# A five-layer network on one core: state-space read-out by 128-row products, and three feed-forward layers that norm behind their first product

## What is computed

```python
def rmsnorm(x, g):
    y = xf * rsqrt(mean(xf * xf, axis=-1) + EPS) * g

def conv_gated_ffn(xn, w_up, conv_w, conv_b, w_down):      # layers 0 to 3; xn = rmsnorm(x, g)
    h = causal_depthwise_conv(xn @ w_up, conv_w, conv_b)   # 3 taps over the tokens
    a, g = split(h, 2)
    return (silu(g) * a) @ w_down                          # ffn4 is the same without the convolution

# s5_layer: the scan gives the states xr, xi of 64 groups; then
y  = einsum('ghp,blgp->blgh', c_re, xr) - einsum('ghp,blgp->blgh', c_im, xi) + d_skip * u
hg = gelu(y) @ w_glu
```

## Time and profile before

| | |
|---|---|
| median of 3 runs | 1708.34 us (1707.26 to 1709.61) |
| the profiled execution's own time | 1710.79 us |
| its span in the profile | 1709.0 us |
| instructions | 29919 |
| mean granted clock of PE | 0.996 of full speed |
| PE, DVE, ACT, POOL busy | 97%, 66%, 53%, 18% |

### The profile page before, as it was taken

One profiled execution on the slowest core, in us unless ns is written; L12 is line 12 of the kernel. 1 busy time (PEld: TensorE's weight loads), 2 busy tenths in 40 slices (PEclk: granted clock), 3 DMA queues, 4 the chain that ended last, 5 costly groups with the idle time before them and its releaser, 6 DMA issues.

```text
span 1709.0 us, 29919 instructions
## 1 busy us (share of the span) xinstructions
PE 1661.0 (97%) x12900; PEld 1529.0 (89%) x12900; DVE 1130.8 (66%) x1578; ACT 904.7 (53%) x1212; POOL 312.7 (18%) x377
## 2 busy tenths in 40 slices
PE   8999999999999998999999999999999999999998
PEld 7989999898999987789998897999988898899998
DVE  5657689856775678567666665766676776645455
ACT  6555554544556657465545555645553755443434
POOL 1212799501370001000000011101006200000000
PEclk9999999999999999999999999999999999999999
DMA  7445547464554554345555433755555632555551
GB/s 253 140 138 171 183 162 247 160 219 148 175 174 158 168 197 140 132 158 188 196 177 170 150 133 112 208 189 181 191 171 153 194 113 90 167 191 182 191 179 49
DMA packets 203395, 286.20 MB, mean 167 GB/s; under 512 B 6432, under 2 KB 162272, under 8 KB 203264
## 3 DMA queue, kind: packets, MB, share of 16 engines
q1 hardware_dynamic: 197584, 272.25, 48.6%
q0 software_dynamic: 2224, 5.75, 1.4%
q10 hardware_dynamic: 3456, 6.29, 1.1%
HBM read 279.03 MB, written 5.24 MB: 166 GB/s over the span
## 4 chain that ended last, share of the span: by engine, by line
PE 89%; DVE 6%; ACT 2%; issue 2%; POOL 1%; DMA 0%; ACTq 0%; SPq 0%; POOLq 0%; DVEq 0%
PE ps L107 88%; DVE wlo L119 2%; ACT arena L113 1%; PE ps L110 1%; ACT whi L113 1%; DVE xres L119 1%; POOL sm L119 1%; DVE arena L119 1%; DVE arena L125 1%; DVE arena L122 0%; DVE sm L122 0%; DVE arena L128 0%; DVE ol L119 0%; DVE arena L137 0%; DMA xres<-in_x 0%
## 5 line engine op out<-in xcount | busy, mean ns | idle before, releaser
L119 DVE TENSOR_TENSOR wlo<-raw,whi 128x2048 fp32r<-128x2048 f32 (+2 forms) x259 | 602.1, 2330 | 259.0 <-ACT whi L113 258.9
L107 PE MATMUL ps<-xh,whi 128*128 128x256 f32 x2296 | 654.7, 285 | 3.8 <-DVE wlo L119 2.4
L107 PE MATMUL ps<-xh,wlo 128*128 128x256 f32 x2296 | 650.5, 283 | 0.0
L107 PE MATMUL ps<-xl,whi 128*128 128x256 f32 x2296 | 650.4, 283 | 0.0
L113 ACT ACTIVATE whi<-raw 128x2048 fp32r<-128x2048 f32 (+2 forms) x259 | 491.9, 1901 | 245.8 <-PE ps L107 242.9
L107 PEld LDWEIGHTS ps<-xh,whi 128*128 128x128 f32 x2296 | 440.3, 192 | 11.0 <-issue 5.0
L107 PEld LDWEIGHTS ps<-xl,whi 128*128 128x128 f32 x2296 | 440.5, 192 | 2.0 <-issue 0.2
L107 PEld LDWEIGHTS ps<-xh,wlo 128*128 128x128 f32 x2296 | 440.3, 192 | 0.1
L107 PE MATMUL ps<-whi,oh 128*128 128x512 f32 (+1 forms) x640 | 249.4, 390 | 0.7 <-ACT arena L113 0.7
L107 PE MATMUL ps<-wlo,oh 128*128 128x512 f32 (+1 forms) x640 | 247.4, 387 | 0.0
L107 PE MATMUL ps<-whi,ol 128*128 128x512 f32 (+1 forms) x640 | 246.8, 386 | 0.0
(11 more groups left out here) (152 smaller groups left out, 1668.6 us busy)
## 6 DMA issues: line engine op xcount, KB each, us to landing
raw<-in_ffn_w_up SPq DMA_DIRECT2D x88, 1024.0 KB, 5.1
raw<-in_ffn_w_down SPq DMA_DIRECT2D x44, 1024.0 KB, 4.9
raw<-in_sb_w_qkv SPq DMA_DIRECT2D x23, 1024.0 KB, 5.5
raw<-in_w_ffn_in SPq DMA_DIRECT2D x22, 1024.0 KB, 5.1
raw<-in_w_in SPq DMA_DIRECT2D x19, 1024.0 KB, 5.1
raw<-in_w_ffn_out SPq DMA_DIRECT2D x11, 1024.0 KB, 5.0
raw<-in_sb_w_o SPq DMA_DIRECT2D x8, 1024.0 KB, 4.9
raw<-in_sg_w_in SPq DMA_DIRECT2D x8, 1024.0 KB, 5.3
```

The costliest lines, as they stand in the source:

```text
L107: return NOP if self.e is None else self.e.matmul(*a, **k)
L119: return NOP if self.e is None else self.e.tensor_tensor(*a, **k)
```

## The change

**Read-out.** y is kept in another order: rows are the four time steps i times 32 features, and the four groups of channels qq stand along the columns. So one product with 128 columns of weights takes the place of four with 32: `read_out` has 4 products with `toep` and 16 with the states. The gelu puts the order right: `gelu(n)` is 16 instructions on 32 rows and 2x64 elements. `gelu(1)` moves from ahead of group 3's work on ACT to behind it, and the load of table `toep` 2 moves up.

**Feed-forwards 2, 3 and 4.** The raw residual is turned (`raw_turn_pe`, 16 transpositions), eight of them ahead of the last bank's sums, four ahead of the first tile and four within it. ACT makes the high parts (`raw_high_act`), DVE the low parts (`raw_low_dve`), the first four ahead of its last addition. The banks are now finished in the order (0,0), (1,0), (0,1), (1,1). The norm's factors are made beside the first tiles; two products turn them into a row (`raw_scale_pe`), ACT copies it, and DVE multiplies each bank of each block by it (`up_scaled`, two instructions of 128x512 a block). The taps read that product and not PSUM, and ACT's first tap waits for it; PE takes a bank again as soon as it is scaled.

The diff, cut to its core:

```diff
@@ feat_major_pair
         for k in range(KT):
+            if st in self.RAW and k == 2:
+                self.raw_turn_pe(pe, st, 1, 1)
             pe.wait_ge(*self.on("xl", st, k))
@@ into_residual
+        if final and st in self.RAW_AFTER:
+            nxt = self.RAW_AFTER[st]
+            for t, j in ((0, 0), (1, 0), (0, 1), (1, 1)):
+                if t == j == 1:
+                    pe.wait_ge(*self.on("x_new", nxt, 1, 0))
+                    for tt in range(2):
+                        self.raw_turn_pe(pe, nxt, tt, 0)
+                part(0, t, j)
+                ins = part(1, t, j)
...
@@ add_residual
+        if nxt in self.RAW:
+            for t, j in ((0, 0), (1, 0), (0, 1), (1, 1)):
+                xs, b = self.x[:, t, j * 512:(j + 1) * 512], self.B[4 + 2 * t + j]
+                if t == j == 1:
+                    self.raw_low_dve(dv, nxt, 0)
+                dv.wait_ge(*(self.on("tile", *key) if t == j == 1 else self.on("sum", st, t, j)))
+                dv.tensor_tensor(xs, b[:, :], xs, ALU.add).then_inc(*self.up("x_new", nxt, t, j))
+            self.raw_low_dve(dv, nxt, 1)
+            return
@@ new
+    RAW = {"ffn2": 40, "ffn3": 56, "ffn4": 72}
+    RAW_AFTER = {"stick1": "ffn3", "second": "ffn4"}
+    def raw_turn_pe(self, pe, st, t, j):
+        pe.wait_ge(*self.on("x_new", st, t, j))
+        for kt in range(4 * j, 4 * j + 4):
+            b, c = self.raw_at(st, kt)
+            ins = pe.transpose(b[:, c + t * P:c + (t + 1) * P], self.x[:, t, kt * P:(kt + 1) * P], self.ident[:, :])
+            if t:
+                ins.then_inc(*self.up("x_turned", st, kt))
+    def raw_high_act(self, ac, st, j):
+        for kt in range(4 * j, 4 * j + 4):
+            b, c = self.raw_at(st, kt)
+            ac.wait_ge(*self.on("x_turned", st, kt | 1))
+            ac.activation(self.xh[:, kt, :], b[:, c:c + 256], ACT_F.Copy, scale=self.gcol(self.RAW[st] + kt)).then_inc(*self.up("xh", st, kt))
+    def raw_low_dve(self, dv, st, j):
+        for kt in range(4 * j, 4 * j + 4):
+            b, c = self.raw_at(st, kt)
+            dv.wait_ge(*self.on("xh", st, kt | 1))
+            dv.scalar_tensor_tensor(self.xl[:, kt, :], b[:, c:c + 256], self.gcol(self.RAW[st] + kt), self.xh[:, kt, :].bitcast(F32),
...
@@ raw_act
+        self.raw_high_act(ac, st, 0)
+        squares(0, 0)
+        squares(1, 0)
+        squares(0, 1)
+        self.raw_high_act(ac, st, 1)
+        squares(1, 1)
@@ raw_scale_pe
+        for t in range(2):
+            pe.wait_ge(*self.on("scaled", st, t))
+            ins = pe.matmul(self.B[3][:, t * P:(t + 1) * P], self.nones[:, :], self.diag(st)[:, t, :], start=True, stop=True)
@@ ffn_pe
+                    if raw and blk == s == 1:
+                        pe.wait_ge(*self.on("r_out", st))
+                    if raw and blk >= 2:
+                        pe.wait_ge(*self.on("up_scaled", l, blk - 2, s))
...
+                    if raw and blk == s == 0:
+                        self.raw_turn_pe(pe, st, 0, 1)
...
+            if raw and blk == 0:
+                self.raw_scale_pe(pe, st)
@@ ffn_act
-                    ac.wait_ge(*self.on("tile", "up", l, s, blk))
+                    ac.wait_ge(*(self.on("up_scaled", l, blk, s) if raw else self.on("tile", "up", l, s, blk)))
@@ ffn_dve
+            if raw and blk == 0:
+                self.cut_lo(dv, ("up", l, 1, 0), 0)
+                self.raw_sums_dve(dv, st)
+                self.cut_lo(dv, ("up", l, 0, 0))
+                self.raw_diag_dve(dv, st)
...
+            if raw and blk < NB:
+                for s in range(2):
+                    dv.wait_ge(*self.on("tile", "up", l, s, blk))
+                    dv.wait_ge(*self.on("r_out", st))
...
+                    dv.tensor_tensor(self.up_scaled()[:, 2 * s:2 * s + 2, :], self.up_bank(blk, s),
+                                     self.raw_scale().unsqueeze(1).to_broadcast([P, 2, 256]), ALU.mult).then_inc(*self.up("up_scaled", l, blk, s))
@@ read_out
-            for i in range(4):
-                for qq in range(4):
-                    pe.matmul(y(qq, i), toep[:, qq, i, :], U4[:, j, qq, :], start=i == 0, stop=False, skip_group_check=True)
+            for qq in range(4):
+                pe.matmul(y(qq), toep[:, qq, :, :].rearrange("p i n -> p (i n)"), U4[:, j, qq, :], start=qq == 0, stop=False, skip_group_check=True)
...
-                    for i in range(4):
-                        for qq in range(4):
-                            ins = pe.matmul(y(qq, i)[:, 1:64], xc[c].rearrange("p a g h -> p a (g h)")[:, 4 * qq + i, :], src[:, qq, c, 0:63],
+                    for qq in range(4):
+                        ins = pe.matmul(y(qq)[:, 1:64], xc[c][:, 4 * qq:4 * qq + 4, :, :].rearrange("p a g h -> p (a g h)"), src[:, qq, c, 0:63],
@@ s5_pe, last tiles
+            if hf:
+                pe.wait_ge(*self.on("x_new", "ffn2", 1, 0))
+                for t in range(2):
+                    self.raw_turn_pe(pe, "ffn2", t, 0)
             glu(hf, 0, 1)
@@ s5_act
-            ac.activation(yT, B[2 + n % 2][:, :].rearrange("p (a b) -> p a b", b=256), ACT_F.Gelu_apprx_tanh).then_inc(*self.up("y_gelu", n))
+            out = yT.rearrange("p a (c i) -> p a c i", i=4)
+            for i in range(4):
+                for qq in range(4):
+                    ins = ac.activation(out[32 * qq:32 * qq + 32, :, :, i], self.s5_y2(n)[32 * i:32 * i + 32, :, qq, :], ACT_F.Gelu_apprx_tanh)
+            ins.then_inc(*self.up("y_gelu", n))
...
-            if j == 3:
-                gelu(1)
...
-            if j % 2 and j != 3:
+            if j % 2:
                 gelu(j // 2)
```

More of the change, by code:

```diff
@@ L401, in part @@
                             w[0][:, k, j * 512:(j + 1) * 512], w[1][:, k, j * 512:(j + 1) * 512], first and k == 0, final and k == 1)
+        if final and st in self.RAW_AFTER:
[7 more added lines that the diff above has]
+                ins = part(1, t, j)
+                if (t, j) != (1, 1):
+                    ins.then_inc(*self.up("sum", st, t, j))
+            ins.then_inc(*self.up("tile", *key))
+            return
         if final:
@@ L481, in gains_dve, with raw_at @@
         dv.tensor_copy(self.gt[:, 0:64], self.B[0][:, 0:64]).then_inc(*self.up("gains"))
+    RAW = {"ffn2": 40, "ffn3": 56, "ffn4": 72}
+    RAW_AFTER = {"stick1": "ffn3", "second": "ffn4"}
+    def raw_at(self, st, kt):
+        return self.B[((4, 5, 6, 7) if st == "ffn2" else (4, 6, 5, 3))[kt // 2]], kt % 2 * 256
+    def raw_turn_pe(self, pe, st, t, j):
[5 more added lines that the diff above has]
+                ins.then_inc(*self.up("x_turned", st, kt))
@@ new lines, in raw_act, with squares @@
+    def raw_act(self, ac, st):
+        ss = self.small("ss" + st, 5)
+        ac.wait_ge(*self.on("gains2" if self.RAW[st] >= 64 else "gains"))
+        def squares(t, j):
+            c = slice(j * 512, (j + 1) * 512)
+            ac.wait_ge(*self.on("x_new", st, t, j))
+            ac.activation(self.jk[:, t, c], self.x[:, t, c], ACT_F.Square, accum_out=ss[:, 2 * t + j:2 * t + j + 1]).then_inc(*self.up("squared", st, t, j))
+        self.raw_high_act(ac, st, 0)
[4 more added lines that the diff above has]
+        squares(1, 1)
@@ L486, with raw_scale_pe, raw_scale @@
+    def raw_scale_pe(self, pe, st):
+        for t in range(2):
+            pe.wait_ge(*self.on("scaled", st, t))
+            ins = pe.matmul(self.B[3][:, t * P:(t + 1) * P], self.nones[:, :], self.diag(st)[:, t, :], start=True, stop=True)
+        ins.then_inc(*self.up("r_turned", st))
+    def raw_scale(self):
+        return self.ar[:, 5120:5376]
     NORM_BANKS = {"stick0": (4, 5, 0, 1, 2, 3, 6, 7), "stick1": (4, 5, 0, 1, 2, 3, 6, 7), "s5": (4, 5, 0, 1, 2, 3, 6, 7),
@@ L2834, in scalar @@
         self.s5_act(ac)
-        self.norm_act(ac, "ffn2", 40)
+        self.raw_act(ac, "ffn2")
         self.ffn_act(ac, 2)
@@ L2839, in scalar @@
         self.stick_act(ac, "stick1")
-        self.norm_act(ac, "ffn3", 56)
+        self.raw_act(ac, "ffn3")
         self.ffn_act(ac, 3, self.nsa_prep_act(ac))
@@ L2863, in vector @@
         self.s5_dve(dv, "ffn2")
-        self.turned_dve(dv, "ffn2", 40)
         self.ffn_dve(dv, 2, "stick1")
@@ L2887, in tensor @@
         self.s5_pe(pe)
-        self.norm_pe(pe, "ffn2")
         self.ffn_pe(pe, 2)
@@ L2891, in tensor @@
         self.stick_pe(pe, "stick1")
-        self.norm_pe(pe, "ffn3")
         self.ffn_pe(pe, 3, self.nsa_prep_pe(pe))
```

69 lines of the change are left out of this document (43 added, 26 removed).

## The result

The changed kernel takes 1719.82 us in the median of 4 runs (1718.60 to 1721.45), the kernel before 1707.80 in the runs beside it: a ratio of 1.0070, 95% interval 1.0052 to 1.0087. That is 12.0 us slower, where 1.0 was forecast, and outside the range of 1703 to 1715. The profiled execution took 1721.45 us with a span of 1719.7, against 1710.79 and 1709.0 before: 10.7 us more.

What follows compares the result with a forecast made beforehand. PE, busy 97% of the span, was taken to bound the kernel. State-space stage +7.7, three starts -6.7, feed-forward bodies nothing: +1.0 us, so a median of 1709.3 us, range 1703 to 1715.

Steps and rivals of the forecast that it cites:

- The read-out: State-space stage, PE: 40 wide records at 0.115 us, 4.6 us a read-out in place of 2.25, 18.8 us more work.
- rival 3: State-space read-outs: the issue gaps stay, five of them, 9.4 us, between 662 and 688; +5.7, 1715.0 us; chance 0.06.
- Rival 1: Read-outs: wide products as cheap as their moving columns, 0.056 us a record, 2.25 a read-out; 1699.6 us; chance 0.13.
- The gelu: State-space stage, ACT: 16 pieces at 0.28 us, 4.5 us in place of 0.6; bounds 0.20 to 0.41 a piece.
- rival 2: Gelus on ACT: dearer pieces, 0.48 us for each 0.01 a piece; at 0.41, +6.2, 1715.5 us; chance 0.15.
- Rival 5: PE's wait at 688: the clock falls, 3.3 us at half speed, +1.7, 1711.0 us; no chance of its own.
- the forecast's own case: Whole kernel: the forecast of 1709.3 us with the clock falling in PE's wait at 688 included; within 0.2%, chance 0.50.
- The stage: State-space stage: 7.7 us longer, with PE waits of 3.7 us near 688 and 2.0 us near 719.
- The three starts: Starts of feed-forwards 2, 3 and 4: 3.0 us each in place of 5.5, 5.3 and 4.9; 6.7 us less.
- The body of the feed-forwards: DVE's two added multiplications of 0.65 us a block cost nothing, hidden in its waits of 1.73 and 1.78 us.
- Rival 4: First feed-forward blocks: DVE falls behind, 2 us a stage for two stages; +4, 1713.3 us; chance 0.06.
- The issue gaps: State-space stage: 10.6 us of PE's gaps, about 128 records apart, are removed as 128 records now last 15 us.

Runs made afterwards that it cites:

- contig: The changed kernel with gelu pieces written side by side; the copy making oh and the subtraction making ol read them in token order: 1712.11 us, 1.0028.
- fill: The changed kernel with unread 128x512 products added, 30 ahead of PE's wait for ol(1), 14 ahead of its wait for gelu 3: 1716.80 us, 1.0046.
- raw_only: The kernel before with the raw residual of the feed-forwards alone, read-out and gelu as before: 1701.99 us, 0.9969.
- the eight forms: Two probes of the changed kernel, each gelu's 16 pieces in another form (stride, partitions, order, function): 0.27 to 0.40 us a piece; 1716.24 and 1713.00 us.
- spread2: The changed kernel with whole gelus, ordered by copies on ACT, DVE, POOL; half tile waits for gelu 2; gelu 1 ahead of group 3's work: 1706.44 us, 0.9990.

## Why the prediction was wrong

The mechanism was the one named, at the two places named. The step that failed is the price of a gelu piece, 0.28 us, where 0.40 was measured; with it the low clock, which the sum put at nothing, cost 4.3 us. The case in which both happen was not priced.

- **The read-out.** 4.6 us by the 0.115 of the earlier trace rows: right, 5.69 with a drive of 1.1 is 4.6, and 4.4 behind a tile. PE was to reach `glu` (0,0,0) at 688.0; it did at 695.56 - 7.10 = 688.46, having entered the stage 0.35 later. No gaps there, right; rival 3 falls. Rival 1 falls too: a record is 0.11 and not 0.056.
- **The gelu: the step that failed.** "16 x 0.28 = 4.5 us", from eight pieces that write side by side. They are 0.40 each. The bound of 0.41 held it, and rival 2 named the right reason to doubt it, a stride of four that no row has, but gave it 0.15. The row had the same size and the wrong form of output. PE's waits are 7.10 and 3.66 in place of 3.7 and 2.0: 5.1 us. With pieces of 0.28 (`contig`) they are 4.54 and 1.74, with 0.8 of the first from the dearer copy and subtraction. The 0.20 a piece that the Trainium skill ("ScalarE: Activation LUTs", What ACT_TABLE_LOAD costs) leads to is half of what was measured; the cheapest form of eight has 0.27.
- **The clock.** Rival 5 set 1.7 us behind one wait, inside the forecast's own case. It came behind both, 7.43 - 5.58 = 1.9 and 5.25 - 2.8 = 2.4 us; `fill` gives 4.3 back. Nothing of it was in the sum. Rival 2 said +6.2 with the clock left at full speed, but dearer pieces make the stands longer, and the two should have been one case: by the measured waits 1709.3 + 5.1 + 4.3 = 1718.7, where 1719.8 was measured.
- **The stage**: 7.7 + 5.1 + 4.3 = 17.1 us, measured 17.2. That it is so close is partly luck: the later read-outs were cheaper by 0.2 each, the tiles dearer by 0.1 to 0.2, and a narrow read-out is 2.35 and not 2.25.
- **The three starts.** -6.7, measured -6.9. Right in sum; the 0.5 us at the second tile is 0.24, and feed-forward 2, where the last addition was to be no later, has 0.55 us of wait for it (762.54 in the trace) that the other two lack.
- **The body of the feed-forwards** at nothing: right, and the waits that were to hide it are those that shrank. Rival 4 falls.
- **The issue gaps.** They went with the fast records, as said, and stayed with them in raw_only, 10.7 us. They come by number of records, which the prediction held against rival 3. The Trainium skill ("Runtime: NRT & Kernel Launch", Instruction fetch mechanics) calls fetching instructions mostly hidden; if the gaps are that, these traces do not agree for records of 14 ns.

## What to carry to other kernels

A duration may be taken from another row only if the output's stride and the order of partitions agree, not just engine and size; where they don't, price the edit at its upper bound first, above all when the instruction stands between an engine and its bound. A wait of PE can cost its length and then slow products behind it, so price both in one case: here 10.8 us of waits brought 4.3 more. And fewer, wider products are no gain where one of them takes longer than the narrow ones that it replaces, here 0.11 us a record against four of 14 ns; look too at what the consumer needs of the new layout.

## What was not expected of the hardware

Small ACT pieces of 32x128 cost 0.27 to 0.28 us or 0.40 by how neighbouring pieces lie to each other, as the eight forms show. PE's clock was at 0.50 after a stand of 0.91 us in spread2, but stayed at 1.00 after one of 1.74 us in contig, and what it cost does not follow the length either: 1.9 us behind 7.10, 1.6 behind 4.54, 2.4 behind 3.66, 2.6 behind 2.37, 1.6 behind 0.91. So the length of the stand alone does not tell. And the gaps between fast records lie at fixed places of the count of records, the same in three kernels.
